# The second head's probabilities of the forgetting branch turned by VectorE squares and DMA instead of by TensorE

## The reference

```
for each block of 128 queries:                    # 8 blocks, 8 heads, keys up to the block's end
    logits = q @ k.T / 8 + (c[t] - c[s])          # c = cumulative log forget gate
    p = softmax(logits masked to s <= t)
    out = p @ v
```

## Time and profile before

| | us |
|---|---|
| median of 3 runs (1348.14 to 1348.27) | 1348.22 |
| the profiled execution, its own time | 1348.53 |
| its span | 1346.7 |
| branch a, steps by squares and DMA (612 to 766) | 154 |
| branch a, the rest (766 to 830) | 64 |

### The profile page before, as it was taken

One profiled execution on the slowest core, in us unless ns is written; L12 is line 12 of the kernel. 1 busy time (PEld: TensorE's weight loads), 2 busy tenths in 40 slices (PEclk: granted clock), 3 DMA queues, 4 the chain that ended last, 5 costly groups with the idle time before them and its releaser, 6 DMA issues.

```text
span 1346.7 us, 20780 instructions
## 1 busy us (share of the span) xinstructions
PE 1326.0 (98%) x7690; PEld 1082.1 (80%) x7690; DVE 771.0 (57%) x1716; ACT 629.4 (47%) x1381; POOL 264.1 (20%) x423
## 2 busy tenths in 40 slices
PE   7999999999999999999999999999999999999998
PEld 6988888777878888887788777787878788888886
DVE  6569866766766875565555555744445354233534
ACT  7467766766754541113443465644454322213223
POOL 3123211002103100003344313323332220000000
PEclk9999999999999999999999999999999999999999
DMA  7054222122214322225555423433544352222522
GB/s 227 24 141 126 71 63 72 50 53 73 72 41 119 99 64 82 80 72 163 162 153 155 141 87 105 127 92 84 156 127 124 119 161 55 78 78 63 188 100 96
DMA packets 146052, 139.54 MB, mean 104 GB/s; under 512 B 13888, under 2 KB 124096, under 8 KB 145696
## 3 DMA queue, kind: packets, MB, share of 16 engines
q0 software_dynamic: 22896, 67.42, 16.9%
q1 hardware_dynamic: 97824, 58.22, 16.0%
q10 hardware_dynamic: 25232, 12.59, 3.2%
HBM read 99.95 MB, written 34.03 MB: 99 GB/s over the span
## 4 chain that ended last, share of the span: by engine, by line
PE 95%; DVE 2%; ACT 1%; issue 1%; POOL 1%; DMA 0%; ACTq 0%; POOLq 0%; DVEq 0%
PE bank L1118 23%; PE bank L1120 23%; PE bank L1119 23%; PE bank L1291 6%; PE slot L1252 6%; PE bank L1264 5%; PE slot L1118 2%; PE slot L1119 2%; PE slot L1120 2%; PE slot L1226 1%; PE bank L1131 0%; DVE slot L1871 0%; ACT yc L1554 0%; DMA iq_st<-iq_hl 0%; PE bank L1177 0%
## 5 line engine op out<-in xcount | busy, mean ns | idle before, releaser
L1118 PE MATMUL bank<-hs,w_hl 128*128 128x512 f32 x1088 | 431.5, 397 | 0.7 <-DVE qa L1814 0.7
L1120 PE MATMUL bank<-hs,w_hl 128*128 128x512 f32 x1088 | 424.3, 390 | 0.0
L1119 PE MATMUL bank<-hs,w_hl 128*128 128x512 f32 x1088 | 423.8, 390 | 0.0
L1651 DVE TENSOR_TENSOR w_hl<-w_raw,w_hl 128x512 fp32r<-128x512 f32 (+1 forms) x168 | 113.6, 678 | 220.7 <-ACT w_hl L1355 219.2
L1120 PEld LDWEIGHTS bank<-hs,w_hl 128*128 128x128 f32 x1088 | 204.2, 188 | 44.0
L1118 PEld LDWEIGHTS bank<-hs,w_hl 128*128 128x128 f32 x1088 | 204.3, 188 | 43.6 <-issue 3.4
L1119 PEld LDWEIGHTS bank<-hs,w_hl 128*128 128x128 f32 x1088 | 204.6, 188 | 39.6
L1355 ACT ACTIVATE w_hl<-w_raw 128x512 fp32r<-128x512 f32 (+1 forms) x168 | 103.9, 621 | 165.1 <-PE bank L1120 155.9
L1678 DVE TENSOR_SCALAR_CACHE_REDUCE idle_out<-score,state 128x768 uint8<-128x768 f32 (+3 forms) x140 | 115.0, 822 | 4.0
L1871 DVE CUSTOM_DVE_ANT_0 slot<-slot,score 128x128 f32<-128x128 f32 (+5 forms) x64 | 47.0, 786 | 50.1 <-PE slot L1252 50.0
L1560 ACT ACTIVATE idle_out<-score,state 128x896 bf16<-128x896 f32 x64 | 69.9, 1093 | 10.0 <-DVE state L1674 8.8
(11 more groups left out here) (338 smaller groups left out, 2415.1 us busy)
## 6 DMA issues: line engine op xcount, KB each, us to landing
w_raw<-in_w_in_dram SPq DMA_DIRECT2D x136, 256.0 KB, 2.9
merged_scratch<-ms POOLq DMA_DIRECT2D x16, 512.0 KB, 3.5
ms<-merged_scratch POOLq DMA_DIRECT2D x16, 512.0 KB, 4.0
square_scratch<-pb ACTq DMA_DIRECT2D x20, 256.0 KB, 2.3
xn<-in_x_dram SPq DMA_DIRECT2D x8, 512.0 KB, 6.6
iq_st<-iq_hl POOLq DMA_DIRECT2D x32, 128.0 KB, 2.8
w_raw<-in_w_o_dram SPq DMA_DIRECT2D x16, 256.0 KB, 4.0
v_scratch<-vtc POOLq DMA_DIRECT2D x6, 512.0 KB, 3.1
```

Of the source, the lines that this page charges most:

```text
L1118: pe.matmul(out_, wh, mh, start=start, stop=False)
L1119: pe.matmul(out_, wh, ml, start=False, stop=False)
L1120: return pe.matmul(out_, wl, mh, start=False, stop=stop)
L1651: v.tensor_tensor(lo, src, hi.bitcast(F32), ALU.subtract).then_inc(w_low, 1)
```

## The change

In the 17 steps the second head's probabilities go the way of the first: DVE turns their squares in place, ACT stores them to a second pair of DRAM scratches, and POOL loads them with four more DMAs. The `turn` entries of these steps become empty: no PE transposes, no ACT copies to `pta`. The entry `square_second` stands behind `exp`. The loads of `ptsa` need four buffers of 4 KiB; the two new ones take the place of `pta`, so the first turned groups after the 17 steps wait for the last of these `pv`. ACT's exponentials of the second head now wait for the store of the second head (`second_stored`); the count that a store waits for (`room`) covers both heads' loads; `pv` waits for eight loads. Branch b's squares are as before.

```diff
-                own = [(x["b"], 0, c) for x in runs[s] for c in range(x["W"] // P)]
+                own = [[(x["b"], hh, c) for x in runs[s] for c in range(x["W"] // P)] for hh in range(HEADS[br])]
+                goal, second = goals[len(squares) % 2], sum(y["br"] == "a" for y in squares)
...
                 plan.append(("exp", runs[s][-1]))
+                if by_dma[s] and br == "a":
+                    step("square_second", unit=runs[s][-1])
...
-        PTQ = {"a": [at(k, f"ptsa{k}", [P, TB, P]) for k in (44, 76)], "b": [at(46, "ptsb", [P, 4, P])]}
+        PTQ = {"a": [[at(k, f"ptsa{k}", [P, TB, P]) for k in pair] for pair in ((36, 40), (44, 76))], "b": [[at(46, "ptsb", [P, 4, P])]]}
...
+            def load_square(u, hh):
+                n, nb = u["square"], u["wide"] // P
+                for j in range(4):
+                    pool.dma_start(PTQ[u["br"]][n % 2][hh][32 * j:32 * j + 32, 0:nb, :].rearrange("a b (i c) -> a (b i) c", i=4),
+                                   square_dram[n % 2 + 2 * hh][0:nb, :, 32 * j:32 * j + 32].rearrange("b (i a) c -> a (b i) c", i=4)
+                                   ).then_inc(square_in[n % 2], 16)
...
+                elif kind == "square_second":
+                    pool.wait_ge(second_stored, 16 * (a["unit"]["second"] + 1))
+                    load_square(a["unit"], 1)
...
-                            pe.wait_ge(square_in[a["square"] % 2], 64 * (a["square"] // 2 + 1))
+                            pe.wait_ge(square_in[a["square"] % 2], a["goal"])
...
+            def store_square(u, hh):
+                n, W = u["square"], u["wide"]
+                if hh:
+                    act.wait_ge(squared_second, u["second"] + 1)
+                else:
+                    act.wait_ge(squared, n + 1)
+                if u["room"]:
+                    act.wait_ge(square_in[n % 2], u["room"])
+                act.dma_start(square_dram[n % 2 + 2 * hh][0:W // P].rearrange("b p c -> p b c"), ...
...
+                        if a["held"]["dma"] and a["br"] == "a":
+                            act.wait_ge(second_stored, 16 * (a["held"]["second"] + 1))
...
+                        if u["br"] == "a":
+                            full(act, u["behind"]["pv"])
...
+                elif kind == "square_second":
+                    u = a["unit"]
+                    own = PR[u["br"]][:, 1, 0:u["wide"]]
+                    dve.wait_ge(slot_free, last_slot(u) + 1)
+                    v.transpose(own, own).then_inc(squared_second, 1)
```

More of the change, by code:

```diff
@@ L57 @@
 SQUARED = {"a": 8, "b": 4}
+HEADS = {"c": 1, "a": 2, "b": 1}
 LAG = {"a": 3, "b": 2}
@@ L277, in square @@
                     x.update(square=len(squares), single=sum(y["slots"] == 1 for y in squares),
-                             moved={part: k for k, part in enumerate(own[:SQUARED[br]])})
+                             moved={part: k for parts in own for k, part in enumerate(parts[:SQUARED[br]])},
+                             wide=min(len(own[0]), SQUARED[br]) * P, room=goal, goal=goal + 64 * HEADS[br], second=second)
                 step("square", unit=runs[s][-1], n=len(squares), before=squares[at] if at >= 0 else None)
@@ L303, in pair_run @@
                 plan.append(("exp", runs[s][-1]))
+                if by_dma[s] and br == "a":
+                    step("square_second", unit=runs[s][-1])
+                elif br == "a":
+                    for x in runs[s]:
+                        x["behind"] = squares[-1]
             x = runs[min(s, n - 1)][-1]
@@ L718, in hybrid_layer_kernel @@
         square_in = [sem(f"square_in{i}") for i in range(2)]
-        square_dram = [nc.dram_tensor(f"square_scratch_{i}", [TB, P, P], F32, kind="Internal").ap() for i in range(2)]
+        squared_second, second_stored = sem("squared_second"), sem("second_stored")
+        square_dram = [nc.dram_tensor(f"square_scratch_{i}", [TB, P, P], F32, kind="Internal").ap() for i in range(4)]
         v_dram = [nc.dram_tensor(f"v_scratch_{i}", [P, T], F32, kind="Internal").ap() for i in range(2)]
@@ L1034, in _ @@
                     pool.wait_ge(square_stored, 16 * (n + 1))
[L1035 to L1038, removed]
+                    load_square(u, 0)
+                elif kind == "square_second":
+                    pool.wait_ge(second_stored, 16 * (a["unit"]["second"] + 1))
+                    load_square(a["unit"], 1)
                 elif kind == "stat_store":
@@ L1284, in _ @@
                             if (a["b"], hh, c) in a["moved"]:
-                                turned = PTQ[a["br"]][a["square"] % 2][:, a["moved"][a["b"], hh, c], :]
+                                turned = PTQ[a["br"]][a["square"] % 2][hh][:, a["moved"][a["b"], hh, c], :]
                             else:
@@ L1500, in _ @@
                         act.wait_ge(square_stored, 16 * a["n"])
-                    if u["held"] is not None and any(part[1] == 0 for part in u["held"]["groups"][0]["parts"]):
+                    if u["held"] is not None and any(part[1] == 0 for grp in u["held"]["groups"][:1] for part in grp["parts"]):
                         full(act, u["held"]["groups"][0]["use"])
@@ L1511, in _ @@
                     if a["held"] is not None:
-                        full(act, a["held"]["groups"][-1]["use"])
+                        for grp in a["held"]["groups"][-1:]:
+                            full(act, grp["use"])
+                        if a["held"]["dma"] and a["br"] == "a":
+                            act.wait_ge(second_stored, 16 * (a["held"]["second"] + 1))
                         if a["held"]["dma"] and not a["dma"]:
@@ L1523, in _ @@
                     if a["dma"]:
[L1524 to L1529, removed]
+                        store_square(a, 0)
+                elif kind == "square_second":
+                    store_square(a["unit"], 1)
                 elif kind == "turn":
```

14 lines of the change are left out of this document (9 added, 5 removed).

## The result

The changed kernel takes **1360.28 us** (median of 4 runs, 1359.73 to 1360.69) against 1348.18 for the kernel before in the same comparison: 12.1 us longer, ratio 1.0089, 95% interval 1.0077 to 1.0101. The forecast was 1344.5, and the range 1340.8 to 1350.8 doesn't hold the time. The profiled execution took 1360.5 us, its span is 1358.7.

The account below looks back on a forecast made before the run. The prediction took PE to bound the kernel (busy 1326.0 of 1346.7 us). 10.8 us won less 2.8, 0.6 and 3.7 lost made 3.7 faster: 1348.2 to 1344.5 us, range 1340.8 to 1350.8.

Parts of the forecast that it names:

- What is removed from PE: 100 transposes leave PE in the 17 steps: 10.8 us won net, 0.108 a part.
- Bank 1 at the steps (2,3): PE's next block waits for bank 1 behind ACT's second store and DVE's second transpose: 2.8 us lost, bounds -0.84 and 4.
- pv of 2.6: This pv, two steps behind, waits for eight loads instead of four: 3.7 us lost, bounds 2.7 and 6.
- The slots: PSUM slots between the steps of 5 and 6, where PE's logits follow the second exponential: 0.6 us lost, bounds 0 and 1.8.
- Nothing lost, if landings stay: Claim that loads other than those of pv of 2.6 arrive in time while landing times stay; stores also lose nothing.
- the loads elsewhere: Loads for the other pv, such as 1.5, arrive in time by 4 us: nothing lost.
- the stores: Second stores land after 4 to 4.5 us, before the next second-head exponential is held up; 1.7 us left: nothing lost.
- The sum of the DMA rows: In the 17 steps the added transfers raise DMA time from 89 to 135 us in some 150: share 0.90 instead of 0.58.
- the rival: The DMA fills up: landings longer by 2.4 us or more make the kernel slower, from 1351 us up; chance 0.17.
- worked example: Landings 4 us longer lose 2.3 us at six logits and 2 more at pv of 2.6: 1360 us.
- The rule on pieces below 512 B: The loads' 128 B pieces might cost twice the stores' price, 156 us in 150, making the DMA the bound; rows disagreed.

Follow-up runs that it names:

- thin_both: The changed kernel with every instruction, wait and issue kept, but the second head's branch-a stores and loads carry one part (64 KB) instead of up to 8: 1345.28 us.
- The mixes: Kernels on no_room moving only 20, 29, 41 or 49 of the 100 parts, the rest turned on PE: 1345.96, 1345.34, 1344.58 and 1349.20 us.
- thin_loads: The changed kernel, but only the second head's loads carry one part, its stores being whole: 1348.08 us.
- thin_stores: The changed kernel, but only the second head's stores carry one part; its whole loads read scratches filled once: 1354.55 us.
- no_room: The changed kernel with a DRAM scratch of its own for each branch-a square, so no store waits for loads of two squares before: 1356.89 us.
- mix_five: no_room with only 49 parts moved, in the steps of (0,1), 4, 5, 6 and 7 without 2.6 and 2.7: 1349.20 us, scattered 1345.52 to 1351.83.
- thin_sp_noise: thin_both (also called the thin kernel) with two extra 384 KB stores behind each of 17 weight loads on SP's queue, nothing waiting for them: 1346.16 us.

## What was right and what was wrong

**What is removed from PE: right.** The distances between the logits of channel 1, from 1.(0,1) to 2.(0,1), in the profiled runs of before and thin_both:

| us | to (2,3) | to 4 | to 5 | to 6 | to 7 | to 2.(0,1) |
|---|---|---|---|---|---|---|
| before | 11.58 | 11.95 | 9.47 | 5.66 | 9.50 | 6.50 |
| thin_both | 10.73 | 12.87 | 8.75 | 5.11 | 8.77 | 5.78 |
| won | 0.85 | -0.92 | 0.72 | 0.55 | 0.73 | 0.72 |
| forecast | 0.84 | -0.33 | 0.72 | 0.61 | 0.72 | 0.72 |

The price of each turned group came true to 0.06 us; bank 1 is the one that didn't. The mixes pay 0.09 to 0.11 us a part. That thin_both as a whole takes 1345.28 us, 0.8 above the forecast, is partly luck: bank 1 cost some 1.5 us more than its term (below), and pv of 2.6 started 1.7 us earlier than forecast, since with small loads POOL's eight issues take 5.15 us instead of 5.96 and PE starts 2.0 us after the last of them begins.

**Bank 1 at the steps (2,3): the moments right, the cost too small.** DVE's low half was forecast to end at 629.3 in channel 0. After has it here:

```profile
626.44 1.11 DVE L1829 STREAM_TRANSPOSE pa<-pa 128x896 f32<-128x896 f32 x1 [0.50 <-ACT pa L1552]
628.63 0.69 DVE L1851 SCALAR_TENSOR_TENSOR qa<-bank,qa 128x512 fp32r<-128x512 f32 x1 [1.07 <-ACT qa L1513]
```

It ends at 629.32. PE's three waits were to be up to 1.9 and twice 0.6 us (the term's own numbers, 0.7 of before and 1.25 and 0.28, make the first 2.2); they are 2.6, 0.9 and 0.9 in thin_both and 7.9 together in after. The loss itself shows in the distances from the logits of (2,3) to those of 4: thin_loads, whose clock doesn't fall in channel 0, loses 1.6, 0.9 and 0.9 us against before, where the term has 1.25 and twice 0.33. So some 1.5 us were missing from this term before any late transfer reached it. In channel 2 of after it is a late load that holds the store ahead of the copy (737.51 above).

**The slots: right without the crowd** (0.2 us of waits in thin_both for 0.6). In after PE waits 2.9 us for slots, 2.6 of them not between 5 and 6 but at the first logits of channel 2, for the store of 8.19 us.

**pv of 2.6: the mechanism right, the size off.** It was to start 8.6 us behind the end of pv of 2.4, cause DMA. PE's timeline around it in after, then in thin_both (pv of 2.4 has 20 matmuls, of 2.5 24, of 2.6 28):

```profile
768.75 1.31 PE L1308 MATMUL bank<-ptsa,va 128*64 128x128 f32 x20
...
775.93 1.53 PE L1308 MATMUL bank<-ptsa,va 128*64 128x128 f32 x24 [2.91 <-issue]
782.43 3.01 PE L1308 MATMUL bank<-ptsa,va 128*64 128x128 f32 x28 [4.97 <-issue]
```

```profile
760.52 1.31 PE L1308 MATMUL bank<-ptsa,va 128*64 128x128 f32 x20
...
764.72 1.53 PE L1308 MATMUL bank<-ptsa,va 128*64 128x128 f32 x24
768.68 2.37 PE L1308 MATMUL bank<-ptsa,va 128*64 128x128 f32 x28 [2.44 <-issue]
```

In after it is 12.4 us (770.06 to 782.43), and pv of 2.5 waits 2.9 as well; PE waits 7.9 us there, where the term was 3.7. In thin_both it is 6.9 us and one wait of 2.4.

**"Nothing lost, if landings stay": the step that failed**, for the loads elsewhere and for the stores. The landings didn't stay: stores of 448 KB 6.1 us instead of 3.7, loads of 112 KB 4.3 instead of 2.9, and single ones 8.19. The sum of the DMA rows that gave a share of 0.90 was right (0.83 to 0.90 measured), and the rival that followed from it, longer landings, names what happened; it got a chance of 0.17. That its worked example also says 1360 us is luck: it took landings 4 us longer and 2.3 us lost at each of six logits. The medians grew by 2.4 and 1.4 us, and the loss lies in four places, at bank 1 twice, at one slot and at pv. The argument that put the rival down was that stores and loads landed early in the earlier trace rows although they overlap. Those rows are from a stretch at 0.58, and the forecast added half as much again to it.

**But the rival's reason was only half of it.** It spoke of the engines' fullness alone. A share of 0.86 made by ACT's extra stores costs the kernel before 1.0 us, not clear of noise. A share of 0.92 in channels 0 and 1, made by stores that nobody waits for, costs the thin kernel 0.2 us at the two places of channel 1 where after loses 6.0 with a lower share. There it costs when the bytes are those of the second head: its store is waited for by ACT's next exponential and by the loads, these by pv and by the store two squares on. In channel 2 and at pv of 2.6, with 8.4 us of the loss, it is shown that these bytes cost (thin_both), but not that others in their place wouldn't. Thin_loads and thin_stores show that stores and loads together cost more than each by itself; that lateness is passed from the one to the other and back fits the chain above and where no_room gained, but how much of the 15 us each link has wasn't measured.

**The clock took some of it.** PE does 10.8 us less work by the forecast, yet is busy only 5.5 us less (1320.5 on the page against 1326.0 in the earlier trace rows). After a wait the granted clock can fall. In after at 1.(2,3):

```profile
676.00:680.00 4.00, 3.29 (x15) 2.40 (x13) 3.46 (x7) 2.53 (x8) 1.25 (x3) 1.00 1.04 267
680.00:684.00 4.00, 1.92 (x6) 1.59 (x7) 1.45 (x3) 1.12 (x2) 3.05 (x4) 0.83 0.94 260
684.00:688.00 4.00, 4.00 (x24) 2.96 (x24) 0.13 (x1) 0.00 (x0) 3.87 (x6) 0.74 1.08 200
```

PE stood for 2.1 of the 4 us from 680; behind that eight matmuls of a block take 0.42 to 0.43 instead of 0.23 us, PE being at the lower of its two levels, 1.2 GHz, some 1.6 us in all. In before the same view of 680 to 684 has a DMA share as high, 1.02, with PE busy throughout and its clock at 1.00. It doesn't follow each wait: at 0.(2,3) PE waits 2.6 us in both kernels, and from 628 to 632 the granted clock is 0.71 in thin_both and 1.00 in after. So a wait of PE can cost more than its length; the forecast had no term for this. The thin_both run has some of it too (busy 1318.5, 7.5 us less than before).

**The rule on pieces below 512 B** (the Trainium skill, DMA: Bandwidth & Descriptors, "Specifications") was set aside because the rows had 3.7 against 3.4 us/MB. On POOL's queue the runs bear that out: 512-byte pieces made its share a MB 6 to 9% smaller. On a hardware queue the trace agrees with the rule's direction: 3.55% a MB against 2.4% on POOL's queue, 1.5 times the price, when SP issued the same loads.

## What to carry to other kernels

A landing time read from a trace holds for the load it was read under: when a change adds half as much again to the DMA engines, look for the landings of a stretch where they are already that full, and put them through each chain that has no slack. Whether a full DMA costs anything is decided by who waits: at two places of channel 1 a share of 0.92 cost 0.2 us with transfers outside the chain, and 0.83 to 0.88 cost 6.0 with large ones inside it. So move only the part of the work whose transfers leave the chains their slack (41 of 100 parts won 3.7 us, 49 lost it, 100 lost 12), and look for the first place where several large transfers meet. A crowd that is added as a test must cover every place where the change lost time; mine ended at 725 us and left channel 2 untested.

## What the chip showed that I hadn't expected

- Landings under load are uneven. In after the median store of 448 KB lands after 6.1 us and one after 8.19; in mix_five one took 10.3, though the share from 752 to 770 us was only 0.69 on the mean. Transfers of 16 and 64 KB in thin_sp_noise, at a share of 0.88, still land after 3.3.
- A DMA issue can hold its engine for longer when others stand just before it. On ACT one took 0.37 us, and up to 1.53 with three stores in a row. On POOL four loads of the kernel before take 2.7 to 3.0 us at a stretch; in after a group of eight stood still for 2.3 us in its midst, the profile doesn't show for what:

```profile
723.99 1.56 POOL L958 DMA_DIRECT2D ptsa<-square_scratch  x2 [1.09 <-DMA square_scratch<-pa]
727.88 4.67 POOL L958 DMA_DIRECT2D ptsa<-square_scratch  x6 [2.33 <-issue]
```

- The same loads in 128-byte pieces cost 1.5 times as much of the engines from SP's hardware queue as from POOL's software queue (3.55% of their time a MB against 2.4%).
